# Last down slab by pairs of chunks, x added one pair ahead, squares behind the copies: one core of Trainium2

## The reference

```
x = x + 0.5 * _swiglu(_rmsnorm(x, ffn1_norm[l]), ffn1_w_gate[l], ffn1_w_up[l], ffn1_w_down[l])
h = _rmsnorm(x, mix_norm[l])
...
x = x + jnp.concatenate([out_a, out_b, out_c], axis=-1) @ w_out[l]
x = x + 0.5 * _swiglu(_rmsnorm(x, ffn2_norm[l]), ffn2_w_gate[l], ffn2_w_up[l], ffn2_w_down[l])
```

```
y = x32 * lax.rsqrt(jnp.mean(x32 * x32, axis=-1, keepdims=True) + RMS_EPS)
return (y * g.astype(jnp.float32)).astype(x.dtype)
```

## Time and profile before

| what | us |
|---|---|
| median of three runs | 4404.97 |
| the three runs | 4387.85, 4404.97, 4408.54 |
| the profiled execution, its own time | 4395.84 |
| its span | 4394.1 |
| TensorE matmuls busy | 4128.5 |
| VectorE busy | 2896.3 |
| ScalarE busy | 1966.5 |
| GpSimd busy | 195.3 |

### The profile page before, as it was taken

One profiled execution on the slowest core, in us unless ns is written; L12 is line 12 of the kernel. 1 busy time (PEld: TensorE's weight loads), 2 busy tenths in 40 slices (PEclk: granted clock), 3 DMA queues, 4 the chain that ended last, 5 costly groups with the idle time before them and its releaser, 6 DMA issues.

```text
span 4394.1 us, 70621 instructions
## 1 busy us (share of the span) xinstructions
PE 4128.5 (94%) x29942; PEld 3799.3 (86%) x29942; DVE 2896.3 (66%) x4335; ACT 1966.5 (45%) x2524; POOL 195.3 (4%) x225
## 2 busy tenths in 40 slices
PE   7989999899998999988988999899999999899998
PEld 6878888788786888877887899899998899899998
DVE  6566675566754667546645699944855699974664
ACT  4445454454543545445424544244444544334443
POOL 0011000110000000001002100000000000000000
PEclk9989999899999999988998999999999999999999
DMA  5523545235454454433542354455653345345654
GB/s 206 183 101 141 187 173 190 99 138 188 157 185 144 144 188 176 163 115 115 187 151 90 116 183 164 142 182 185 249 189 139 130 169 183 137 166 187 236 197 144
DMA packets 118603, 716.08 MB, mean 163 GB/s; under 512 B 13953, under 2 KB 19729, under 8 KB 37009
## 3 DMA queue, kind: packets, MB, share of 16 engines
q1 hardware_dynamic: 90864, 660.64, 42.2%
q10 hardware_dynamic: 26400, 43.28, 2.9%
q0 software_dynamic: 1024, 7.64, 0.4%
HBM read 690.38 MB, written 21.13 MB: 162 GB/s over the span
## 4 chain that ended last, share of the span: by engine, by line
PE 75%; DVE 15%; ACT 5%; issue 2%; DMA 2%; POOL 1%; ACTq 1%; POOLq 0%; DVEq 0%; SPq 0%
PE psum L701 21%; PE psum L630 13%; PE psum L632 12%; PE psum L631 12%; PE psum L702 11%; DVE slab_low L1870 4%; DVE room L2521 3%; ACT slab_high L1390 2%; DVE room L2518 1%; DVE x L1992 1%; DVE room L2542 1%; PE psum L1048 1%; POOL room L2574 1%; DVE room L2536 1%; PE psum L1031 1%
## 5 line engine op out<-in xcount | busy, mean ns | idle before, releaser
L1870 DVE TENSOR_TENSOR slab_low<-slab,slab_high 128x2048 fp32r<-128x2048 f32 x622 | 1430.5, 2301 | 814.9 <-ACT slab_high L1390 812.2
L1390 ACT ACTIVATE slab_high<-slab 128x2048 fp32r<-128x2048 f32 x630 | 1186.7, 1884 | 520.3 <-PE psum L702 264.6
L701 PE MATMUL psum<-h_parts,slab_high 128*128 128x512 f32 x2816 | 1000.1, 400 | 44.1 <-DVE h_parts L2179 38.8
L630 PE MATMUL psum<-h_parts,slab_high 128*128 128x256 f32 x2880 | 845.3, 294 | 35.5 <-DVE h_parts L2179 23.1
L631 PE MATMUL psum<-h_parts,slab_high 128*128 128x256 f32 x2880 | 827.4, 287 | 0.0
L632 PE MATMUL psum<-h_parts,slab_low 128*128 128x256 f32 x2880 | 826.8, 287 | 0.0
L702 PE MATMUL psum<-h_parts,slab_low 128*128 128x256 f32 x2816 | 792.4, 281 | 0.0
L630 PE MATMUL psum<-hidden_parts,slab_high 128*128 128x256 f32 x2368 | 671.2, 283 | 18.1 <-DVE hidden_parts L2550 5.6
L701 PEld LDWEIGHTS psum<-h_parts,slab_high 128*128 128x128 f32 x2816 | 532.6, 189 | 178.3 <-issue 32.5
L632 PE MATMUL psum<-hidden_parts,slab_low 128*128 128x256 f32 x2368 | 664.9, 281 | 0.0
L631 PE MATMUL psum<-hidden_parts,slab_high 128*128 128x256 f32 x2368 | 664.5, 281 | 0.0
(11 more groups left out here) (330 smaller groups left out, 4523.8 us busy)
## 6 DMA issues: line engine op xcount, KB each, us to landing
slab<-in_up SPq DMA_DIRECT2D x176, 1024.0 KB, 4.8
slab<-in_keys_up SPq DMA_DIRECT2D x128, 1024.0 KB, 4.8
slab<-in_keys_down SPq DMA_DIRECT2D x128, 1024.0 KB, 4.8
slab<-in_down SPq DMA_DIRECT2D x88, 1024.0 KB, 4.8
slab<-in_w_in SPq DMA_DIRECT2D x16, 1024.0 KB, 4.8
slab<-in_wq SPq DMA_DIRECT2D x16, 1024.0 KB, 4.8
peer_gates<-room ACTq DMA_DIRECT2D x64, 256.0 KB, 2.0
room<-peer_gates ACTq DMA_DIRECT2D x64, 256.0 KB, 4.4
```

Of the source, the lines that this page charges most:

```text
L630: nc.tensor.matmul(out, lhs[0], rhs[0], start=first, stop=False, **options)
L701: nc.tensor.matmul(out, lhs[0], rhs, start=first, stop=False, **options)
L1390: nc.scalar.activation(k.high[m % PARTS][:, 0:width], k.slabs[m % RING][:, 0:width], ACT.Copy).then_inc(k.rounded.up())
L1870: nc.vector.tensor_tensor(k.low[m % RING][:, 0:width], k.slabs[m % RING][:, 0:width], k.high[m % PARTS][:, 0:width], ALU.subtract).then_in ...
```

## The change

Five things change.

1. In the last slab of a down projection of ffn and peer, TensorE goes by pairs of output chunks: for pair j both hidden rows, then the next pair, and raises `pair_done` behind each of the first three pairs. The wait for the last hidden row now stands ahead of the slab. The products of mixer_one, conv, nsa and fox keep their order, and get the three signals in their last chunk.
2. The additions of `add_down` wait pair by pair for `pair_done`, the last one for the slab.
3. `early_input` on VectorE adds pair j + 1 ahead of the remainders of pair j.
4. ScalarE makes the square of a pair directly behind its two copies.
5. ScalarE's wait ahead of the copies is for the last slab but one of the stage before (`inputs_free`), except behind stick. The root of the plain norm stage moves to another place in SBUF, so that the next stage's squares don't overwrite it.

```
+        self.inputs_free = self.slab_done.start - (before != "stick")
...
         for r in range(FC // 2):
             high, low = self.take()
+            if r == FC // 2 - 1:
+                nc.tensor.wait_ge(k.hidden_ready.sem, k.hidden_ready.at(FC))
+                for j, e, c in itertools.product(range(DC // 2), range(2), range(2)):
+                    cols = slice(e * D + (2 * j + c) * P, e * D + (2 * j + c + 1) * P)
+                    mm = self.product_wide(k.banks[2 * j + c].rearrange("p (a t) -> p a t", a=2), (high[:, cols], low[:, cols]),
+                                           k.hidden[:, 2 * r + e], False, e == 1)
+                    if e == 1 and c == 1 and j < 3:
+                        mm.then_inc(k.pair_done.up())
+                mm.then_inc(k.slab_done.up())
+                break
...
@@ mixed_half, mixed_quarter
+            if chunk == DC - 1 and c in (1, 3, 5):
+                mm.then_inc(k.pair_done.up())
...
@@ expert_down
+        if r == ROUNDS - 1:
+            if e == 1:
+                return
+            for j, e, c in itertools.product(range(DC // 2), range(2), range(2)):
...
@@ ScalarE.ffn, ScalarE.early_input
-            nc.scalar.wait_ge(k.slab_done.sem, k.slab_done.start)
+            nc.scalar.wait_ge(k.slab_done.sem, k.inputs_free)
...
-        for j in range(DC // 2):
+            if c % 2 == 0:
+                continue
+            j = c // 2
             nc.scalar.activation(v.square[:, 2 * j:2 * j + 2, :], k.x[:, 2 * j:2 * j + 2, :], ACT.Square).then_inc(k.squared.up())
...
@@ VectorE.add_down
-            if j == 0:
+            if j < 3:
+                nc.vector.wait_ge(k.pair_done.sem, pair_done[j])
+            else:
                 nc.vector.wait_ge(k.slab_done.sem, all_done)
...
@@ VectorE.early_input
+        self.finish(0)
         for c in range(DC):
-            if c % 2 == 0:
-                self.finish(c // 2)
+            if c % 2 == 0 and c + 2 < DC:
+                self.finish(c // 2 + 1)
```

More of the change, by code:

```diff
@@ L605, in norm_stage_views @@
     v = Views()
-    norm_views(k, v)
+    v.square = k.carve(DC, T)
+    k.taken = 4 * DC * T
+    v.rstd = k.carve(T)
     return v
@@ L759, in ffn @@
                     mm = self.product_wide(k.banks[c].rearrange("p (a t) -> p a t", a=2), (high[:, cols], low[:, cols]), k.hidden[:, f],
-                                           f == 0, f == FC - 1)
-                    if f == FC - 1 and c in (1, 3, 5):
-                        mm.then_inc(k.pair_done.up())
+                                           f == 0, False)
             mm.then_inc(k.slab_done.up())
@@ L992, in mixed_half @@
                               j == 0 and e == 0 and c % 2 == 0, j == DC // 2 - 1 and e == 1, skip_group_check=True)
+            if j == DC // 2 - 1 and e == 1 and c in (1, 3, 5):
+                mm.then_inc(k.pair_done.up())
         if e == 1:
@@ L1352, in expert_down @@
         at = FIRST_HIDDEN + 2 * (r % 2) + e
+        if r == ROUNDS - 1:
+            if e == 1:
+                return
+            for j, e, c in itertools.product(range(DC // 2), range(2), range(2)):
+                cols = slice(e * D + (2 * j + c) * P, e * D + (2 * j + c + 1) * P)
+                mm = self.product(k.banks[j][:, c * T:(c + 1) * T], (high[:, cols], low[:, cols]),
+                                  (k.hidden[:, at + e, 0, :], k.hidden[:, at + e, 1, :]), False, e == 1, skip_group_check=True)
+                if e == 1 and c == 1 and j < 3:
+                    mm.then_inc(k.pair_done.up())
+            mm.then_inc(k.slab_done.up())
+            return
         for c in range(DC):
@@ L1356, in expert_down @@
                               (k.hidden[:, at, 0, :], k.hidden[:, at, 1, :]),
-                              r == 0 and e == 0 and c % 2 == 0, r == ROUNDS - 1 and e == 1, skip_group_check=True)
+                              r == 0 and e == 0 and c % 2 == 0, False, skip_group_check=True)
         if e == 1:
@@ L1939, in add_down @@
         k, nc = self.k, self.k.nc
-        all_done = k.slab_done.at(slabs)
+        pair_done, all_done = [k.pair_done.at(j + 1) for j in range(3)], k.slab_done.at(slabs)
         def finish(j):
             both = k.x[:, 2 * j:2 * j + 2, :]
-            if j == 0:
+            if j < 3:
+                nc.vector.wait_ge(k.pair_done.sem, pair_done[j])
+            else:
                 nc.vector.wait_ge(k.slab_done.sem, all_done)
```

## The result

The changed kernel is faster. Its median is 4331.42 us (4321.6 to 4338.24, four runs), that of the kernel before on the same chip 4399.06 us (4387.85 to 4408.54, four runs). The ratio is 0.985, with a 95% interval of 0.9833 to 0.9868: 67.6 us less. The forecast was 4361 us with a range of 4340 to 4387, so the direction was right and the gain lies beyond the fast end. In a second comparison the same kernel stood at 4334.5 us against 4397.02 (0.9864, 0.9847 to 0.9882). The forecast was counted from the 4404.97 us of the three runs known then; with the fourth run the kernel before stands 5.9 us lower, so 6 of the 30 us between 4361 and 4331 are not the gain's. Counted from either, the gain is more than forecast.

What follows compares the result with a forecast made beforehand. The kernel was taken as TensorE-bound, with gains only in pauses at hand-overs: 17.2 us for chunks, 23.8 for squares and 3 for clock, 44 in all, so 4404.97 − 44 = 4361 us, range 4340 to 4387.

Steps and rivals of the forecast that it cites:

- What bounds the kernel: TensorE's matmuls are busy 4128.5 of 4394.1 us; the change can pay only in its pauses at hand-overs, ceiling 74 us.
- The three rows of GpSimd's sum: TensorE's 8 waits at hand-overs for GpSimd's sum of squares, 23.8 us together, were all to go.
- The remainder's waits: TensorE's waits at hand-overs for VectorE's remainder of the stage input, 68.1 us, were to fall by some 17 us.
- The end: At the end of the kernel three of four adds run under the last slab, saving 1.6 us of wait.
- Signals: A signal per pair starts the first add 1.33 us earlier behind add_down stages, 2.3 behind nsa, nothing behind feed-forward.
- kind B: Hand-over where the stage before projects by add_down, 7 times in the program: one add of 0.68 us per pair.
- Holds: GpSimd's adds, now between VectorE's remainders, delay these by 0.5 to 2.3 us; gain 41 us, without holds 51.
- Rival 2: No holds on the path, or without harm: 51 us plus up to 12 of clock, 4342 to 4354 us; chance 0.13.
- rival 3: Following stages, bound by their own chains, take back half the gain: 18 us remain, 4387 us; chance 0.13.
- rival 4: GpSimd's adds always get ahead of VectorE: 58 us held against 51 gained, 24 of clock, 4436 us; chance 0.04.
- the clock term: Fewer pauses at hand-overs mean less TensorE time at 1.2 GHz: 3 us taken, bounds 0 and 12, or −5.
- fox's row: After fox's 5.64 us pause TensorE runs ten microseconds at granted clock 0.50; up to 4.4 us could come back.

## Why the prediction was right and where it was wrong

**What bounds the kernel:** right. TensorE's pauses at hand-overs were the place, and their groups went about as read. The three rows of GpSimd's sum, 23.8 us, are gone whole. The remainder's waits fell by 13.6 us, forecast 17.2 − 1.6 = 15.6. The end gained 1.7 in its wait, forecast 1.6. Together 39.1 us for 41. What the sum left out is that some of it comes back: the time without work fell by 33.9 us in the first profile of the changed kernel and 27.0 in the second.

**Signals:** right in size. The first add of kind B has no idle time before it; after nsa it comes 2.1 us earlier, where 2.3 was taken. Alone the signals give 8 us (interval 2 to 15), where the terms of the prediction for them are 10.6.

**Holds:** right. Remainders of up to 1.52 us appeared, 26 us of VectorE's time. Most of it lies beside TensorE's work: by the run with GpSimd held back 6.8 us are on its path, where the forecast took 51 − 41 = 10. Rival 2, no holds, falls by the rows, though its time was nearer. The Trainium skill, SBUF — State Buffer, "Who interferes with whom", gave the rule for it, and holding GpSimd back (all remainders at about 479 ns) agrees with it. But the rule was no reason to undo the overlap: the held kernel is 15 to 22 us slower.

**Half taken back later** (rival 3): fell as a whole, but its mechanism is there in the peers. Between first adds, fox is 10.7 us shorter and conv 8.1 (143.1 to 135.1), more than the 6.6 and 5.5 + 1.3 us of pauses that were to go there; the second mixer, bound by its own chain, is 10.9 shorter. nsa's stage is longer (241.0 us before, 243.5 after between the same first adds), and its clock fell from 0.90 to 0.87. The first peer hardly gained: 881.2 us before, 880.0 and 883.6 in the two profiles after, though its sum of squares came earlier (the second peer, 881.9 us, is 9.1 and 5.8 shorter). The wait for VectorE's one-hots is 5.4 and 10.2 us longer in these profiles, which is about what is missing between 39.1 us of named pauses and 33.9 and 27.0 us of time without work. The prediction put this at nothing ("all these chains begin with the root that needs the sum"); it is 5 to 12 us, not half of the gain. That the change causes it rests on these rows; no run isolates it, and with the signals alone the wait is 44.4 us.

**Slower** (rival 4): fell. GpSimd's adds do get in between, but not on TensorE's path often enough.

**The step that failed is the clock term:** "The bounds are 0 and 12 us (a stretch less at each of several hand-overs), and below nothing too … I take 3, nearest to fox's row." For fox it was right: its ten microseconds at 0.50 are down to one stretch of 3.4 us, worth 3.4 us. But the term was priced at that one row, as if the other pauses had no clock behind them. What it measured can be put between several numbers. Half of the 273.8 − 240.7 = 33.1 us at the lower level is 16.5 us, in one profile each; counting only what TensorE was busy of it, half of 221.3 − 190.9 is 15 us, and 22 by the second profile of the changed kernel. TensorE's busy time fell by 23.6 us in the first pair. The runs give 25 us at most by (1 − c), and 14 us by the 0.55 that runs of one kernel show. So it is 14 to 25 us, beyond the upper bound of 12. The rest of the runs' time, without the (1 − c) part, fell by 36 to 42 us: the 41 us of the sum for the pauses stand. In the first pair of profiles 33.9 us of time without work and 16.5 of clock leave 7 of the 57.5 us unassigned. 41 us and the middle of that clock range would have given about 4344 us, inside the range.

The Trainium skill has the rule that would have carried this as a rival of its own. TensorE: Matmul & The Clock Gate, "A second HAM failure mode: psum-queue depth-cycling", says of another kernel that frequent short idle times between groups of matmuls let the clock swing between its levels, and that throughput is lost by it between the bursts. The trace agrees: the five stretches at the lower level in the first peer of the kernel before (from 2729.6, 2777.4, 2814.9, 2852.5 and 2876.4 on) have as the nearest pause ahead of them one of only 1.8 to 2.1 us, and removing 5 to 6 us pauses in two places and pauses of 1 to 3 us elsewhere took seven of 44 stretches away.

What stays open: why a given pause is followed by a stretch at the lower level in one profile and not in another. Behind the 2.77 us of the earlier trace rows the kernel before shows none, while the changed kernel has one of 6.8 us from 561.6 on, and its second profile has none there either. Of the 33.1 us at the lower level that went between the two profiles, 20.6 lie in the two peers, over 260 us behind their hand-overs, and in the profiles of all kernels here the peers' part goes from 0 to 44 us. So only averages over runs carry the clock's share here, not single places.

## What to carry to other kernels

In a kernel that TensorE bounds at 95%, price a pause twice: once for itself, and once for the clock behind it. Here the second price, 14 to 25 us, was a third to almost two thirds of the first, so the sum of waits alone came out too low. To learn how large it is, fill the pauses with products that nobody reads and time that kernel, before anything is moved. Look also at what the next chain does with an earlier start: here the waits for the peers' one-hots were 5 to 10 us longer. And a longer instruction on VectorE (26 us of holds) is no cost until TensorE waits for it.

## What was not expected of the hardware

- Forty unread products made the kernel before 13 us faster (0.997, 0.9958 to 0.9982).
- A net 4.4 us of pauses put back, by the named rows, went with 15 to 22 us of time, with the mean granted clock of the runs going from 0.9745 to 0.9705.
- Gains of clock needn't show: with the plain norms filled, the stretch behind the first norm was 2.2 us shorter and the mean granted clock of the runs was 0.977, the highest of all, and the time was the same.
- A stretch at 1.2 GHz can stand behind a single pause of 2 us, as five do in the first peer.
